# Both products of the first feed-forward block by seven block products in place of eight, with the blocks between them kept in DRAM

## What is computed

```python
h = layer_norm(DEEPNORM_ALPHA * h + mix, ln1_g[i], ln1_b[i])
ff = jnp.square(jax.nn.relu(h @ w_ff1[i])) @ w_ff2[i]      # 1024x1024 @ 1024x4096, then 1024x4096 @ 4096x1024
h = layer_norm(DEEPNORM_ALPHA * h + ff, ln2_g[i], ln2_b[i])
```

## Time and profile before

| what | value |
|---|---|
| three runs | 2627.62, 2629.1, 2640.84 us, median 2629.1 |
| profiled execution, span from first to last instruction | 2634.6 us |
| PE busy | 2556.0 us (97%) |
| DVE, ACT, POOL busy | 1533.7, 793.5, 189.3 us |
| feed-forward block, first product's first matmul to the next block's | about 361.5 to 1093 us |
| share of the chain that ended last, by engine | PE 91%, DVE 5%, ACT 2% |

### The profile page before, as it was taken

How to read it: one execution, slowest core, us unless ns; L and a number is a source line. 1 busy time by engine, 2 the same in 40 slices (tenths; PEclk the granted TensorE clock), 3 DMA queues, 4 the chain that set the end, 5 groups by cost and what they waited for, 6 DMA issues and landing times.

```text
span 2634.6 us, 32495 instructions
## 1 busy us (share of the span) xinstructions
PE 2556.0 (97%) x12496; PEld 2120.1 (80%) x12496; DVE 1533.7 (58%) x2345; ACT 793.5 (30%) x1353; POOL 189.3 (7%) x94
## 2 busy tenths in 40 slices
PE   8999999999999999998999999999999999999998
PEld 6777887888888888787888888887788888888886
DVE  6668365444444446656355588888566464646466
ACT  2245041110111011446334465554532121212122
POOL 6303400000000000000222200000000000000000
PEclk9986999999999999998999999998999999999999
DMA  4401603322332234013111001021012121212011
GB/s 123 36 9 64 94 28 96 94 84 80 96 94 83 74 98 127 17 54 111 33 35 35 27 23 33 17 97 41 17 56 65 32 64 32 64 32 66 29 56 72
DMA packets 201576, 157.05 MB, mean 60 GB/s; under 512 B 56184, under 2 KB 176512, under 8 KB 201472
## 3 DMA queue, kind: packets, MB, share of 16 engines
q1 hardware_dynamic: 183344, 124.94, 16.6%
q10 hardware_dynamic: 18128, 30.71, 4.4%
HBM read 147.23 MB, written 11.56 MB: 60 GB/s over the span
## 4 chain that ended last, share of the span: by engine, by line
PE 91%; DVE 5%; ACT 2%; issue 1%; DMA 1%; SPq 0%; ACTq 0%; DVEq 0%
PE pd L818 26%; PE pd L820 26%; PE pd L819 26%; PE pt L1338 1%; PE pd L1385 1%; PE pt L1416 1%; PE pd L1307 1%; PE pt L1400 1%; PE pt L818 1%; PE pt L1355 1%; PE pt L1418 1%; PE pt L838 1%; PE pt L820 1%; PE pt L819 1%; PE pt L1357 1%
## 5 line engine op out<-in xcount | busy, mean ns | idle before, releaser
L818 PE MATMUL pd<-actT_hi,st_hi 128*128 128x512 f32 x1872 | 749.9, 401 | 7.1 <-DVE st_lo L2233 3.7
L820 PE MATMUL pd<-actT_hi,st_lo 128*128 128x512 f32 x1872 | 734.2, 392 | 0.0
L819 PE MATMUL pd<-actT_lo,st_hi 128*128 128x512 f32 x1872 | 733.7, 392 | 0.0
L818 PEld LDWEIGHTS pd<-actT_hi,st_hi 128*128 128x128 f32 x1872 | 354.6, 189 | 78.1 <-ACT evac L1573 4.0
L820 PEld LDWEIGHTS pd<-actT_hi,st_lo 128*128 128x128 f32 x1872 | 354.1, 189 | 76.1
L819 PEld LDWEIGHTS pd<-actT_lo,st_hi 128*128 128x128 f32 x1872 | 354.7, 189 | 66.9
L818 PE MATMUL pd<-mv_hi,hid_hi 128*128 128x512 f32 x864 | 337.8, 391 | 3.5 <-DVE acc L2548 1.5
L819 PE MATMUL pd<-mv_lo,hid_hi 128*128 128x512 f32 x864 | 336.9, 390 | 0.0
L820 PE MATMUL pd<-mv_hi,hid_lo 128*128 128x512 f32 x864 | 336.7, 390 | 0.0
L1704 ACT ACTIVATE mv_hi<-raw 128x1024 fp32r<-128x1024 f32 x54 | 55.9, 1056 | 602.0 <-PE pd L820 478.1
L1573 ACT ACTIVATE evac<-pd 128x1024 f32<-128x1024 f32 x76 | 77.9, 1025 | 452.6 <-PE pd L820 452.6
(11 more groups left out here) (340 smaller groups left out, 3761.4 us busy)
## 6 DMA issues: line engine op xcount, KB each, us to landing
raw<-in_w_ff SPq DMA_DIRECT2D x64, 512.0 KB, 3.9
ada_raw<-in_w_ada ACTq DMA_DIRECT2D x64, 384.0 KB, 3.2
raw<-in_w_up SPq DMA_DIRECT2D x44, 512.0 KB, 3.8
raw<-in_w_in SPq DMA_DIRECT2D x30, 512.0 KB, 3.7
raw<-in_w_down SPq DMA_DIRECT2D x22, 512.0 KB, 3.3
acc<-in_x SPq DMA_DIRECT2D x16, 512.0 KB, 8.6
raw<-in_w_out SPq DMA_DIRECT2D x12, 512.0 KB, 3.4
raw<-in_w_ple_gate SPq DMA_DIRECT2D x8, 512.0 KB, 3.8
```

Of the source, the lines that this page charges most:

```text
L818: pe.matmul(out_ap, a_hi, b_hi, start=start, stop=False, skip_group_check=check)
L819: pe.matmul(out_ap, a_hi, b_lo, start=False, stop=False, skip_group_check=check)
L820: return pe.matmul(out_ap, a_lo, b_hi, start=False, stop=stop, skip_group_check=check)
```

## The change

A product of two matrices cut into 2x2 blocks is made of 7 block products instead of 8, with sums of blocks before and after (Winograd's form). P1 to P7 are the block products.

**First product.** The weight matrix is taken in 16 pairs of 256 columns (`FF`, 112 block products). Each block product is 12 matmuls, 4 contracted blocks by three passes. The sums of the activations T1 to T4 are made once, on the second half of the turned rows, by DVE and POOL (`second_half_turned`, `turned_sums`). The sums of the weights are made per pair by POOL (`weight_sum`, 4 instructions of 128x512). ACT rounds each block into a ring of five, DVE subtracts (`block_lo`). P1 and P2 of a pair share a bank, so do P6, P7 and P4, and P5 and P3; between two uses of a bank DVE (or ACT, for P1) takes out what is in it (`pair_out`, five per pair, one input in PSUM). ACT does relu and square. POOL makes four sums of the squared blocks (`hid_sums`). Seven blocks per pair go to DRAM (`hid_stores`, 7 x 256 KB).

**Second product.** It is no longer spread over the chunks but follows the first: 7 long products of 16 steps, 112 steps. A step loads one 256 KB block back (`s_load`), loads or uses a 128x512 block of `w_ff2`, which now stays in SBUF in four quarters of 16 blocks (`quarter_load`), splits both (ACT `long_hi`, DVE `long_lo`, two instructions), and has 12 matmuls. POOL makes the sums of the weights in place (`long_sum`, 64 instructions of 128x512). The result of a long product is added to one, two, three or four quarters of `acc` (`long_add`, 52 of 128x512), during the steps of the next one. The norm of rows 0 to 3 and their turning move into the last two long products.

The steps of the six vectors are now at eight of every twelve block products (`ada_at`, from product 9 on to 100), the residual in 32 halves of a row at three of every seven (`RES`, products 16 to 87). The loops are written out, not in hardware loops. Removed are `ff_chunk`, `ff_tiles`, `ff_rows` and `ff_units`. The core of the diff:

```diff
+def seven_products(n):
+
+    order = [(0, "P1"), (1, "P1"), (0, "P2"), (1, "P2")]
+    order += [(p, name) for p in range(2) for name in PART_B]
+    order += [(p, name) for p in range(2, n) for name in ("P1", "P6", "P2", "P7", "P5", "P4", "P3")]
+    return order, {at: g for g, at in enumerate(order)}
+
...
+LONG = ("P1", "P2", "P5", "P6", "P3", "P7", "P4")
+
+ADDS = {"P1": ((0, 0), (0, 1), (1, 0), (1, 1)), "P2": ((0, 0),), "P5": ((0, 1), (1, 1)),
+        "P6": ((0, 1), (1, 0), (1, 1)), "P3": ((0, 1),), "P7": ((1, 0), (1, 1)), "P4": ((1, 0),)}
+
...
+        def bank_of(p, name):
+            if name in ("P1", "P2"):
+                return pd[:, 1, p % 2 * HB:(p % 2 + 1) * HB]
+            if name in ("P5", "P3"):
+                return pt[:, p % 2, :]
+            return pd[:, 0, p % 2 * HB:(p % 2 + 1) * HB]
+
...
+        def ada_at(g):
+
+            i, n = (g - ADA0) // 12, (g - ADA0) % 12
+            return 8 * i + n if g >= ADA0 and n < 8 and i < 8 else None
...
+                pool.wait_ge(w_sum, 4 * p + SUM[name] - 1)
+                if name == "S3":
+                    pool.tensor_tensor(a21, a11, a21, ALU.subtract).then_inc(w_sum, 1)
+                elif name == "S2":
+                    pool.wait_ge(bk_lo, AT[p, "P1"] + 1)
+                    pool.tensor_tensor(a11, a22, a21, ALU.subtract).then_inc(w_sum, 1)
+                else:
+                    pool.wait_ge(bk_lo, AT[p, "P2"] + 1)
+                    pool.tensor_tensor(a12, a12, a11, ALU.subtract).then_inc(w_sum, 1)
+
+            def hid_sums(p):
+                pool.wait_ge(hid_rdy, 4 * p + 4)
+                for n, (kind, out_, a, b, op) in enumerate((("s1", hs1, h21, h22, ALU.add), ("s3", h21, h11, h21, ALU.subtract),
+                                                            ("s2", hs2, h22, h21, ALU.subtract),
+                                                            ("s4", hs4, h12, hs2, ALU.subtract))):
+                    if n:
+                        pool.wait_ge(hs_sum, 4 * p + n)
+                    if p:
+                        pool.wait_ge(hid_st[kind], 16 * p)
+                    pool.tensor_tensor(out_[:, :], a[:, :], b[:, :], op).then_inc(hs_sum, 1)
...
+                b12, b22 = turned_h[:, 2 * i % 4, :], turned_h[:, (2 * i + 1) % 4, :]
+                pool.wait_ge(tp_hi, job + 2)
+                pool.wait_ge(t1_sum, i + 1)
+                pool.tensor_tensor(b12, b22, b12, ALU.subtract).then_inc(t_sum, 1)
+                pool.wait_ge(t_sum, 3 * i + 1)
+                pool.wait_ge(t_lo, T_LO["B22", i])
+                pool.tensor_tensor(b22, b22, h0_f[:, i, :], ALU.subtract).then_inc(t_sum, 1)
+                pool.wait_ge(t_sum, 3 * i + 2)
+                pool.tensor_tensor(h0_f[:, 4 + i, :], h0_f[:, 4 + i, :], b22, ALU.subtract).then_inc(t_sum, 1)
...
+                    pool.tensor_tensor(q0, q1, q0, ALU.subtract).then_inc(q_sum, 1)
+                elif name == "T2":
+                    pool.wait_ge(*landed(3, k))
+                    pool.wait_ge(f2_lo, 2 * (2 * 16 + k + 1))
+                    pool.tensor_tensor(q0, q3, q0, ALU.subtract).then_inc(q_sum, 1)
+                elif name == "T4":
+                    pool.wait_ge(q_sum, 16 + 3 * k + 1)
+                    pool.tensor_tensor(q2, q2, q0, ALU.subtract).then_inc(q_sum, 1)
+                else:
+                    pool.tensor_tensor(q1, q3, q1, ALU.subtract).then_inc(q_sum, 1)
...
+            def pair_product(g):
+                p, name = FF[g]
+                bank = bank_of(p, name)
+                a_hi, a_lo = ring(g, P)
+                pe.wait_ge(bk_lo, g + 1)
+                if name == "P1":
+                    if p < 2:
+                        pe.wait_ge(m_free, 15 if p == 0 else 16)
+                    else:
+                        pe.wait_ge(ev_x, p - 1)
+                elif name == "P2":
+                    pe.wait_ge(ev_s1, p + 1)
+                elif name == "P6" and p >= 2:
+                    pe.wait_ge(ev, 5 * (p - 2) + EV["21"])
+                elif name == "P7":
+                    pe.wait_ge(ev, 5 * p + EV["U2"])
+                elif name == "P5" and p >= 2:
+                    pe.wait_ge(ev, 5 * (p - 2) + EV["12"])
+                elif name == "P4":
+                    pe.wait_ge(ev, 5 * p + EV["U3"])
+                elif name == "P3":
+                    pe.wait_ge(ev, 5 * p + EV["22"])
+                first = name in ("P1", "P6", "P5")
+                for k in range(4):
+                    if p == 0 and name in T_OF:
...
+            def long_free(i):
+
+                if i == 0:
+                    pe.wait_ge(ev, 5 * (NF - 1) + EV["21"])
+                    pe.wait_ge(ev_x, NF)
+                elif i == 1:
+                    pe.wait_ge(ev, 5 * NF)
+                    pe.wait_ge(mod_rdy, 1)
...
+                    pe.wait_ge(f2_add, ADD_TO[LONG[i - 2]])
...
+            def long_step(s):
+                pe.wait_ge(f2_lo, 2 * (s + 1))
+                if s % 16 == 0:
+                    long_free(s // 16)
...
+                for r in range(4):
+                    last = long_passes(s, r)
+                last.then_inc(f2_done, 1)
...
+            def block_hi(g):
+                p, name = FF[g]
+                if g >= BLOCKS:
+                    act.wait_ge(pr_done, g - BLOCKS + 1)
+                act.wait_ge(*a_ready(p, name))
+                act.activation(ring(g, P)[0], a_block(p, name), ACT.Copy).then_inc(bk_hi, 1)
+
...
+            def long_hi(s):
+                s_raw_, s_hi, _ = s_slot(s)
+                act.wait_ge(*s_free(s))
+                act.wait_ge(s_in[s % BLOCKS], 16 * (s // BLOCKS + 1))
+                act.activation(s_hi, s_raw_, ACT.Copy).then_inc(f2_hi, 1)
+                if s >= 4:
+                    act.wait_ge(f2_done, s - 3)
...
+                    act.wait_ge(ev, 5 * NF)
+                if s < 4:
+                    act.wait_ge(ada_mm, 8)
+                act.wait_ge(*w2_ready(s))
+                act.activation(t_ring[s % 4][0][:, :], q_slot(W2_OF[LONG[s // 16]], s % 16), ACT.Copy).then_inc(f2_hi, 1)
...
+            def block_lo(g):
+                p, name = FF[g]
+                a_hi, a_lo = ring(g, P)
+                dve.wait_ge(bk_hi, g + 1)
+                dve.tensor_tensor(a_lo, a_block(p, name), a_hi.bitcast(F32), ALU.subtract).then_inc(bk_lo, 1)
...
+            def second_half_turned():
+                for i in range(5):
+                    if i < 4:
+                        dve.wait_ge(tp_hi, TPJ["h1"] + 8 + 2 * i + 1)
+                        dve.tensor_tensor(h0_f[:, i, :], turned_h[:, 2 * i % 4, :], h0_f[:, i, :], ALU.subtract)\
+                            .then_inc(t1_sum, 1)
+                        odd[0] += 1
+                        dve.wait_ge(tp_odd, odd[0])
+                        dve.tensor_tensor(actT_lo[:, 4 + i, HB:S], turned_h[:, (2 * i + 1) % 4, :],
+                                          actT_hi[:, 4 + i, HB:S].bitcast(F32), ALU.subtract).then_inc(t_lo, 1)
+                    if i:
+                        t_low("T2", i - 1)
+                        t_low("T4", i - 1)
+                    if i < 4:
+                        t_low("T1", i)
+                        t_low("T3", i)
+                dve.sem_inc(tp_lo, 8)
...
+            def pair_out(g):
+
+                p, name = FF[g]
+                bank, s1 = bank_of(p, name), s1_c[:, p % 2, :]
+                if name in ("P1", "P2"):
+                    return
+                dve.wait_ge(pr_done, g + 1)
+                if name == "P6":
+                    dve.wait_ge(ev_s1, p + 1)
+                    dve.wait_ge(ev, 5 * p)
+                    dve.tensor_tensor(u2[:, :], bank, s1, ALU.add).then_inc(ev, 1)
+                elif name == "P7":
+                    dve.wait_ge(ev, 5 * p + EV["U2"])
+                    dve.tensor_tensor(u3[:, :], bank, s1, ALU.add).then_inc(ev, 1)
+                else:
+                    kind, out_, other = {"P5": ("22", h22, u3[:, :]), "P4": ("21", h12, s1), "P3": ("12", h21, u2[:, :])}[name]
+                    dve.wait_ge(ev, 5 * p + EV[kind] - 1)
+                    if p:
+                        dve.wait_ge(hs_sum, 4 * p)
+                        dve.wait_ge(hid_st[{"22": "22", "21": "12", "12": "s3"}[kind]], 16 * p)
+                    dve.tensor_tensor(out_[:, :], bank, other, ALU.add).then_inc(ev, 1)
...
+            for g in range(1, NP + 1):
+                m = ada_at(g)
+                if m is not None:
+                    if m and m % 8 == 0:
+                        mod_cols(m // 8 - 1)
+                    ada_step(m // 8, m % 8)
+                pair_out(g - 1)
+                if g + 4 < NP:
+                    block_lo(g + 4)
+                if g in RES:
+                    residual(RES.index(g))
+
+            def long_lo(s):
+                s_raw_, s_hi, s_lo = s_slot(s)
+                t_hi_, t_lo_ = t_ring[s % 4]
+                dve.wait_ge(f2_hi, 2 * s + 1)
```

(23 more changed lines are left out.)

600 lines of the change are left out of this document (442 added, 158 removed).

## The result

The changed kernel takes 2705.7 us (median of 4 runs, 2701.38 to 2712.56); the kernel before takes 2635.0 us beside it. The ratio is 1.0261, 95% interval 1.0223 to 1.0299: 2.6% or 71 us slower. Forecast were 2643 us and a range of 2590 to 2685. The direction was right, the size was not. The profiled execution took 2701.38 us, with a span of 2699.1 us.

The account below looks back on a forecast made before the run. PE's matmuls were taken to bound the kernel. -87 + 21 + 40 + 31 + 11 - 2, DMA 0, made +14 us on a median of 2629.1: 2643 us, range 2590 to 2685.

Parts of the forecast that it names:

- Matmuls, -87: Both products: 384 fewer matmuls at 0.227 us each save 87 us.
- Start, +21: Start of first product: PE waits 21 us while DVE and POOL alternate on splits and activation sums.
- First product, +40: First product: POOL's sums hold DVE, 28.3 us of work against 21.8 in eight products; 40 us lost in all.
- POOL needs 1.5 us or more: Sign for POOL's 512-column instructions, priced at 1.20 us: if 1.5 or more, the loss is larger than told.
- `ring_lo` at 1 to 1.8 us: Sign in first product: DVE's weight-block subtraction averages 1 to 1.8 us instead of 0.69, held by POOL.
- DMA, 0: Transfers in both products stay hidden, costing 0; vector loads land in 3.2 us, within the time of two products.
- Transfers become the bound: Rival: vector loads landing in 5 us or later beside 1 MB loads lengthen vector steps; +10, 2653 us, chance 8%.
- Clock, +11: PE's clock drops after waits: 1.2 us in each of six stretches and 4 at the start, 11 us.
- The clock falls at each short wait: Rival: one 1.7 us drop per 12 to 15 us of loosened work, +35 rather than +11; 2667 us, chance 15%.
- ACT has 16 instructions of 0.6 us per pair, 9.6 of 19: hidden.: First product: ACT's 9.6 us of work per 19 us pair is hidden and adds nothing.
- The residual: First product: residual halves on DVE at 0.61 us each, 3.4 of them in the eight products with vector steps.
- Second product, +31, end -2: Second product: waiting sums cost 22 us, with other terms 31; at the end, norms and the old last chunk's waits, -2.

Follow-up runs that it names:

- e10: e9 with six products between residual rows, and the sums at the start and in the second product moved from POOL to DVE: ratio 1.0134 to the kernel before.
- e8: Changed kernel without 62 of 64 vector loads, vector steps after the first eight narrowed to one column: ratio 1.0055 to the kernel before.
- e2: Changed kernel with 62 of the 64 vector loads left out, all steps still computed: ratio 1.0113 to the kernel before.
- e9: Changed kernel with three vector-load buffers instead of two, rel_bias copies later and second-product blocks loaded ahead: ratio 1.0068 to the kernel before.
- e6: Changed kernel without 62 of 64 vector loads, POOL's first-product sums narrowed to one column after the first pair: ratio 0.9952 to the kernel before.
- e14: e10 with all sums on DVE, many later, steps spread, takings first, weight pairs loaded earlier, residual moved: 2600.7 us, ratio 0.9857 to the kernel before.
- e7: e5 plus rel_bias copies later and six products between each eighth residual half and the next: ratio 1.0103 to the kernel before.
- e5: Changed kernel with vector loads issued before weight blocks, and second-product blocks 5 to 8 ahead of the last four stores: ratio 1.0192 to the kernel before.
- e1: Changed kernel with ACT's two rel_bias copies issued after the first norm's second row instead of before: ratio 1.0224 to the kernel before.

## Why the prediction was wrong

Summed between the same events, from the old profile to the new one, the forecast had +14 us and +65.6 were measured (the next block's first such matmul came at 1117.0 and then at 1182.6 us). By its terms:

- **Matmuls, -87.** Right: 384 fewer, and 12 start in 2.72 us wherever nothing waits and the clock is full. PE is busy only 50 us less, since many last longer (see the clock).
- **Start, +21.** Right in kind and size: forecast 38.4 us from the first matmul to the taking of P6 (6.2 + 33 - 0.8), 42.4 with its 4 of the clock, measured 41.2. DVE and POOL alternate as in the earlier trace rows; PE waits 15.6 us in 4 for `t_lo` and 4.4 for a block. With the 12 sums on DVE it is 3.9 us shorter (e10). The turns (timeline):

```profile
387.03 1.61 POOL L1068 TENSOR_TENSOR turned_h<-turned_h,h_f 128x512 f32<-128x512 f32 x1
387.43 1.77 DVE L2692 TENSOR_TENSOR actT_lo<-h_f,actT_hi 128x512 fp32r<-128x512 f32 x1
388.72 1.59 POOL L1070 TENSOR_TENSOR h_f<-h_f,turned_h 128x512 f32<-128x512 f32 x1
```

- **First product, +40.** The size of the term held: POOL's sums cost 39.0, 32.3 or 26.7 us by the three ways above, within the range of 20 to 61. Its working did not, and that the size came out is in part luck. It added 1.02 us of hold per sum to DVE's work, 28.3 us for eight products with steps that last 21.8; the sums held DVE 0.49 us each, DVE was busy 17.9 to 23.0 us in each of the eight passages from the first to the last of eight steps, 171 of their 223 us, and taking the steps' work away gave 12.8 us (e8), not all of the 40. The sums also stood in ACT's line, 62.4 us, which the prediction did not cost. The sign "POOL needs 1.5 us or more" came true (1.55), "`ring_lo` at 1 to 1.8 us" nearly (0.93). For the stage the forecast comes to 348 us (291 of block products, 10 of small matmuls, 40, and 7 of the clock for six stretches) and 386.8 came. Most of these 39 us are the next step's.
- **"DMA, 0 ... Vector loads land in 3.2 us and have two products, 5.4 us, less DVE's 1.06."** This is the step that failed. The time allowed was right, some 4.3 us: most loads are issued as DVE's step ends. The landing time was right for loads by themselves (3.3 us) and not for the 17 issued within 5 us after a 1 MB load of weights (6.5 in the median, up to 11.0), and eight of these make DVE stand, PE behind it, and, since the next load waits for DVE's step in ACT's list, ACT with all that it rounds. The term put at nothing cost 36.9 us (e2); a third buffer gives back 26.9 of them (e9). The rival *Transfers become the bound* had this mechanism, loads of 5 us or later beside 1 MB loads, and gave it 8% and +10 us, on the ground that DVE would use half the time for POOL's holds anyway; e6 shows the two costs to be nearly separate. The price, not the idea, was wrong there. How much of the 36.9 us is the landing and how much the ring stays open.
- **Clock, +11.** More came. Matmuls that start over 0.25 us after the one before, with no wait between, add up to 2.5, 20.8 and 9.4 us over 0.227 each in the three stages, against 4.9 in the old block (361.5 to 1062 us): +28. The rival *The clock falls at each short wait* had +35 at 15%. It is not a loss beside those of the other terms: the slow stretch shown above follows a wait, and with fewer waits there is less of it (6.1 us in the first product of e14), so what an edit gives back includes it.
- **"ACT has 16 instructions of 0.6 us per pair, 9.6 of 19: hidden."** Its busy time was right (144.9 us in the stage, for 107 block products) and says nothing on when it gets to an instruction: it waited 62.4 us for POOL's sums and 50.4 for DVE's takings in the stage.
- **The residual**, costed at 0.61 us per half, brought a load that the prediction did not look at: each row of 256 KB is issued by ACT one product before its use. 12.4 us of waits, 14.0 in e7. With the three buffers it was worth nothing (359.9 to 359.3), so it is not a cost that adds to the others.
- **Second product, +31, end -2.** Together 6 us more than forecast: 384.7 us from 797.9 to 1182.6, against 379 (755.5 from 361.5 to 1117.0 in the old profile, + 14, less the 42.4 and 348 above). The handover from the first product, costed at nothing, was 13.2 us (e5), the sums cost 14.4 and not 24, and 2 are left over. The two errors nearly cancel, which is luck. The prediction looked at the 0.5 MB per step and not at the order in which SP issues it.
- **Ahead of the block, 0.** 8.4 us there. The change removed two loads on ACT, and the copies behind them moved up against SP's. That the copies hold up the weights is shown (e1); that the removal is why they do so more than before is not.

The miss by the profiles is some 52 us (65.6 less 14): 39 in the first product, 8 ahead of it, 6 in the second product and the end, less 1 at the start. The forecast in absolute time missed by 63; 6 of the rest are the kernel before, 2629.1 us when the forecast was made and 2635.0 beside the changed one. The direction was right, at a chance of 0.50, and not for the predicted reasons alone: vector loads, handover and late weights, all three put at nothing, make 58.5 of the 65.6 us if they are added up, and without them the change would lie within the 0.5% that the prediction called no change. The prediction costed the length of a transfer by itself, not beside others and not by its place in a queue.

The rule of the Trainium skill on the exclusive lock ("SBUF — State Buffer", section "SBUF: two separate sides") is borne out by the start: 1.77 us for DVE's instruction of 0.69 while POOL has one of 1.6, so a hold of 1.08. The 2.5 cycles an element of the Trainium skill ("GPSIMD Engine Reference", section 2.1) give 1.07 us, an estimate; the hold agrees with it, while the instruction alone takes 1.27 to 1.30 in the trace.

## What to carry to other kernels

When work is moved into the shadow of a bound engine, cost every load by its landing time beside the largest load of the same stretch (here 6.5 us, not 3.3), from the moment at which its issuing queue reaches it and its buffer is free; a ring of two buffers makes the issuer stand for the consumer. A sum belongs on the engine that can afford to stand for its operand, or at a step where the operand has long landed: the same 64 sums on DVE made the second product 37 us longer at one place (344.6 to 381.2, e9 to e10) and 11 us shorter at another (333.6, e14). And cut both traces at common events before a cause is sought: losses in four places looked like one.

## What was not expected of the hardware

- Two copies of 0.02 MB in 4112 packets on ACT's queue: beside them four 256 KB loads from SP's queue take 17.4 us in the median to land; without them beside it they took 5.8 (e1). The packets in the DMA view of the changed kernel from 225 to 325 us (packets, MB, share of 16 engines):

```profile
q10 hardware_dynamic: 4112, 0.02, 7.8%
```

- POOL's instruction of 128x512 on two SBUF inputs shows 1.27 to 1.30 us alone and 1.6 in turns with DVE, but holds DVE for only 1.08 where the two meet. Since many do not meet, a sum on POOL cost DVE 0.49 us in the mean in the first product (58 us for 118), and 0.61 when it makes it itself.
- With one column in place of 512 POOL's sums still took 0.46 us each in e6 (53.10 us for 116).
